# Passing weight strips through the ring of gathered rows, and keeping output and selection strips

## The chip, the cores and the metric

One NeuronCore of one Trainium2 chip runs the whole program. The metric is the time of one execution on the device in microseconds (us), here the median of the runs. TensorE is called PE, VectorE DVE, ScalarE ACT, GpSimd POOL and SyncE SP, as in the profile.

## The reference

Two layers work on 512 tokens of 1024 numbers (float32). Each layer adds a token mixer and then a channel mixer to the residual stream:

```
h = h + mixer(rms_norm(h))          # layer 0: gated linear attention, layer 1: sliding-window attention
h = h + peer_ffn(rms_norm(h))
```

A mixer is a set of projections with fixed weights around attention. The channel mixer picks, for every token and each of 8 heads, 16 of 16384 experts by a product-key search and computes, over its 128 picks e with gate g,

```
out[t] = sum_e  gelu(u[e] . x[t]) * g[t,e] * v[e]
```

Nearly all bytes come from this: each of 512 tokens reads 128 pairs (u, v) of 8 KB in each layer.

## The kernel before

The 512 tokens are four blocks of 128, so there are eight stages: four blocks in layer 0, four in layer 1. A stage serves the picks of one block while the other engines prepare the next block (its mixer, projections and expert search). That preparation is called a *prep*; it is of kind "gla" in layer 0 and "swa" in layer 1.

**Rows.** One pick of all 128 tokens is a *row*: a gather of 128 x 8 KB = 1.049 MB from the table into one slot of `ring`, which has nine slots (SLOTS). POOL issues the gathers (L666). DVE takes the dot product with h (L1094), ACT computes gelu and the coefficient (L1357, L1360) and, for most rows, a diagonal matrix (L1368), with which PE adds the v half to `acc` (L1723); for the rest of the rows DVE adds it to `side` (L1085). Whoever adds it raises the semaphore `used` of the slot, and POOL may gather the row that comes nine later. A stage has 128 rows, called row 0 to 127 below.

**Beats.** Every engine's program is one stream in which the pieces of the prep stand between rows. The table AT (not changed) says for each piece before which row, called its beat, an engine does it: for a gla prep PE does q0 at 12, q1 24, k0 29, k1 38, v0 to v3 at 43 to 52, r0 to r3 at 56 to 62, out0 to out3 at 71 to 79, pq0 to pq3 at 84 to 105; for a swa prep q0 to q3 at 13 to 22, kv 25, out0 to out3 at 75 to 87, pq0 to pq3 at 93 to 112. The prep that runs in stage 0 has later beats of its own. `beside` and `serve` weave the two. A piece whose input is late holds the rows behind it on that engine.

**Strips.** The weights of the projections are cut into strips of 256 columns, 1.049 MB each like a row: in layer 0 twenty (q0, q1, k0, k1, v0 to v3, r0 to r3, out0 to out3, pq0 to pq3, numbered 0 to 19), in layer 1 thirteen (q0 to q3, kv, out0 to out3, pq0 to pq3). "out" strips are the mixer's output projection, "pq" strips the queries of the expert search. Each is needed once in every block. Strips 0 to 8 of a layer stay in `resident` (nine places, RESIDENT). The others, 9 to 19 in layer 0 and 9 to 12 in layer 1, are fetched again for each block into a buffer of their own, `stream`, which holds one strip, in two halves (CUTS): SP issues a half (L559) as soon as PE has used the same half of the strip before. At the start of the program the ring is still empty, and strips 9 to 17 of the first block lie in it.

**SP's order.** SP issues in one order, with its waits between: streamed strips with the bias, the norm gain (after "oT") and the keys (after "y") among them (`load_streamed`, L536 on), the next block's x (`load_block`), the result of the stage before (`close`). Layer 1's resident strips come in two parts: five during stage 2 after the prep's last streamed strip (`load_kept_ahead`), four in stage 3 (`load_kept_rest`).

PE's use of a strip is in `left`, `right` and `query` (L1460, L1514, L1481); `strip`, `cut_loaded` and `cut_done` hold its waits and signals.

## Time and profile before

| | |
|---|---|
| median of 3 runs | 2897.97 us (2896.73 to 2898.08) |
| the profiled execution | 2902.58 us, its span 2900.4 us |
| PE matmul busy | 2284.9 us, 79% of the span |
| DVE busy | 2184.6 us, 75% |
| POOL busy | 1244.1 us, 43% |
| ACT busy | 1183.7 us, 41% |
| bytes by DMA | 1170.27 MB, mean 403 GB/s |
| gathered rows | 1024, 1073.81 MB, 89.7% of the DMA engines' time |
| DMAs issued by SP | 94.74 MB, 8.3% |

The span runs from the first to the last instruction of the program. A busy share is an average over the span and says nothing of when. "DMA share" is the mean busy share of the 16 DMA engines; GB/s is what they moved in a stretch. Times in the views count from the start of the span.

### The profile page before, as it was taken

How to read it: one execution, taken by the hardware profiler on the slowest of the kernel's cores; microseconds unless marked ns; L12 is line 12 of the kernel's file. 1: busy time of each engine (PE TensorE's matmuls, PEld its weight loads, DVE VectorE, ACT ScalarE, POOL GpSimd, SP SyncE). 2: the span in 40 equal slices, each digit the busy share in tenths (PEclk: the TensorE clock that was granted, in tenths of full speed). 3: DMA queues.
4: the chain of work that ended last, by engine and by line, in shares of the span. 5: the costliest groups of instructions: out<-in, count | busy, mean ns of one | idle time of the engine just before them, and what ended most of it. 6: DMA issues, size and time to landing. Idle time of an engine off the chain costs nothing.

```text
span 2900.4 us, 27200 instructions
## 1 busy us (share of the span) xinstructions
PE 2284.9 (79%) x7394; PEld 1213.3 (42%) x7394; DVE 2184.6 (75%) x5166; ACT 1183.7 (41%) x3457; POOL 1244.1 (43%) x1049
## 2 busy tenths in 40 slices
PE   9779787788877887786887878877788878886567
PEld 8536442454424554243443434443354434432122
DVE  2688678876878757796688876988679876887664
ACT  3154334344343443445344453435534453433333
POOL 0254335443444333444434543354434444345655
PEclk9899999899999898998899988989889998988989
DMA  6599999999999999999999999999999999999998
GB/s 271 209 418 421 398 398 416 421 421 403 415 420 421 420 375 420 420 418 421 421 393 406 422 421 420 389 416 421 421 402 406 421 421 421 399 421 421 422 422 350
DMA packets 170817, 1170.27 MB, mean 403 GB/s; under 512 B 19668, under 2 KB 19928, under 8 KB 36136
## 3 DMA queue, kind: packets, MB, share of 16 engines
q0 software_dynamic: 147456, 1073.81, 89.7%
q1 hardware_dynamic: 23208, 94.74, 8.3%
q8 instruction: 58, 0.95, 0.1%
q14 instruction: 95, 0.78, 0.1%
HBM read 1164.28 MB, written 4.19 MB: 403 GB/s over the span
## 4 chain that ended last, share of the span: by engine, by line
DMA 28%; DVE 14%; PE 11%; issue 6%; POOL 3%; ACT 3%; POOLq 0%; DVEq 0%; ACTq 0%
DMA ring<-in_uv,pick 26%; PE acc L1723 6%; DVE ring L1094 4%; POOL ring L666 3%; PE ps L1514 3%; DVE side L1085 1%; DMA xc<-h 1%; DMA stream<-in_strips 1%; ACT diag L1368 1%; DVE arena L969 1%; DVE arena L950 1%; DVE arena L1040 1%; DVE arena L1044 1%; DVE arena L951 1%; DVE arena L1031 1%
## 5 line engine op out<-in xcount | busy, mean ns | idle before, releaser
L666 POOL DMA_INDIRECT ring<-in_uv,pick x1024 | 1239.7, 1211 | 1630.5 <-PE acc L1723 1092.9
L1723 PE MATMUL acc<-ring,diag 128*128 128x512 f32 x2988 | 1542.5, 659 | 465.3 <-ACT diag L1368 462.3
L1094 DVE CUSTOM_DVE_ANT_0 ring<-ring,h_now 128x1024 f32<-128x1024 f32 x1024 | 1235.4, 1222 | 490.2 <-DMA ring<-in_uv,pick 474.0
L1723 PEld LDWEIGHTS acc<-ring,diag 128*128 128x128 f32 x2988 | 582.6, 207 | 1287.7 <-ACT diag L1368 702.8
L1357 ACT ACTIVATE gelu<-dots 128x1 f32<-128x1 f32 x1024 | 206.1, 201 | 1264.6 <-DVE dots L1094 1258.0
L1085 DVE SCALAR_TENSOR_TENSOR side<-ring,coef,side 128x1024 f32<-128x1024 f32 x270 | 346.0, 1281 | 23.1 <-ACT coef L1360 23.0
L1360 ACT ACTIVATE coef<-gate,gelu 128x1 f32<-128x1 f32 x1024 | 302.0, 295 | 33.2
L1368 ACT ACTIVATE diag<-ident,coef 128x128 f32<-128x128 f32 x747 | 300.1, 402 | 29.8 <-PE acc L1723 5.5
L1514 PE MATMUL ps<-resident,actT 128*128 128x256 f32 x896 | 220.3, 403 | 14.5 <-ACT actT L1169 14.5
L1514 PEld LDWEIGHTS ps<-resident,actT 128*128 128x128 f32 x896 | 178.1, 202 | 58.9 <-issue 18.2
L1481 PE MATMUL ps<-actT,stream 128*128 128x128 f32 x960 | 124.9, 291 | 23.6 <-DMA stream<-in_strips 22.7
L1481 PEld LDWEIGHTS ps<-actT,stream 128*128 128x128 f32 x960 | 121.2, 205 | 43.9 <-DMA stream<-in_strips 31.5
L1514 PE MATMUL ps<-stream,actT 128*128 128x256 f32 x336 | 96.7, 446 | 50.0 <-DMA stream<-in_strips 47.2
L1514 PEld LDWEIGHTS ps<-stream,actT 128*128 128x128 f32 x336 | 73.2, 224 | 79.4 <-DMA stream<-in_strips 62.5
L1357 ACT ACT_TABLE_LOAD x77 | 98.8, 1283 | 1.4
L1094 DVE DVE_READ_ACCUMULATOR2_ANT dots<- 128x1 f32 x1024 | 83.8, 82 | 0.0
L1305 ACT ACTIVATE arena<-ps 128x256 f32<-128x256 f32 x31 | 11.8, 381 | 126.6 <-PE ps L1481 126.6
L1460 PEld LDWEIGHTS ps<-actT,resident 128*128 128x128 f32 x512 | 59.1, 193 | 5.0 <-issue 4.5
L1460 PE MATMUL ps<-actT,resident 128*128 128x128 f32 x512 | 60.6, 277 | 0.0
L1425 PE MATMUL ps<-ident,arena 128*128 128x128 f32 x224 | 38.2, 318 | 27.6 <-DVE arena L711 15.2
L1425 PEld LDWEIGHTS ps<-ident,arena 128*128 128x128 f32 x224 | 29.9, 163 | 50.4 <-issue 26.6
L687 DVE TENSOR_SCALAR stat<-stat 128x1 f32<-128x1 f32 (+2 forms) x24 | 3.8, 160 | 61.3 <-ACT actT L1186 28.0
(198 smaller groups left out, 1454.6 us busy)
## 6 DMA issues: line engine op xcount, KB each, us to landing
stream<-in_strips SPq DMA_DIRECT2D x102, 512.0 KB
resident<-in_strips SPq DMA_DIRECT2D x18, 1024.0 KB, 12.9
ring<-in_uv,pick POOLq DMA_INDIRECT x1024
ring<-in_strips SPq DMA_DIRECT2D x9, 1024.0 KB, 19.6
arena<-in_keys SPq DMA_DIRECT2D x8, 512.0 KB
xc<-in_x SPq DMA_DIRECT2D x4, 512.0 KB
h<-arena SPq DMA_DIRECT2D x4, 512.0 KB, 11.4
xc<-h SPq DMA_DIRECT2D x4, 512.0 KB
```

The source lines that it names most:

```text
L666: pool.indirect_dma_start(ring[:, n % SLOTS, :], None, tables[layer], bass.IndirectOffsetOnAxis(ap=pick[:, col:col + 1], axis=0),).then_in ...
L950: step.mark(dve.max_index(topi[:, v, 0:8], top[:, v, 0:8], score(i)))
L1085: dve.scalar_tensor_tensor(side[:], ring[:, slot, D:2 * D], coef[:, slot:slot + 1], (side if began else xc)[:], ALU.mult, ALU.add).then_in ...
L1094: dve.tensor_tensor_reduce(ring[:, slot, 0:D], ring[:, slot, 0:D], h_now[:], 1.0, 0.0, ALU.mult, ALU.add, dots[:, slot:slot + 1]).then_inc ...
L1357: act.activation(gelu[:, slot:slot + 1], dots[:, slot:slot + 1], ACT.Gelu).then_inc(gelued, 1)
L1360: act.activation(coef[:, slot:slot + 1], gate[:, col:col + 1], ACT.Copy, scale=gelu[:, slot:slot + 1]).then_inc(weighed, 1)
L1368: act.activation(diag[:, turn % 4, :], ident[:], ACT.Copy, scale=coef[:, slot:slot + 1]).then_inc(diag_ready, 1)
L1425: i = pe.transpose(ps[:, bank + k // 4, (k % 4) * P:(k % 4 + 1) * P], src[:, k, :], ident[:])
L1460: i = pe.matmul(ps[:, bank, (2 * side + c) * P:(2 * side + c + 1) * P], w[:, k, c * P:(c + 1) * P], actT[:, k, :], start=(k == 0), stop=(k ...
L1481: i = pe.matmul(ps[:, 2 + c, (j % 2) * P:(j % 2 + 1) * P], w[:, k, c * P:(c + 1) * P], actT[:, k, :], start=(k == 0), stop=(k == KT - 1))
L1514: i = pe.matmul(dst, actT[:, k, :], w[:, k, :], start=(k == 0 and bias is None), stop=(k == KT - 1))
L1723: m = pe.matmul(acc[:, b * 512:(b + 1) * 512], diag[:, turn % 4, :], ring[:, slot, D + b * 512:D + (b + 1) * 512], start=(r == 0 and i == ...
```

## The change

`stream` and its semaphores go. The place that it had becomes a tenth place of `resident`. KEPT says which strips stay: in layer 0 v3 (7), r3 (11), out0 to out3 and pq0 to pq3; in layer 1 all but q0 to q2. The strips that don't stay (PASSING) are given places among the rows in one order over the whole program (`ring_order`): each stands one row ahead of its beat. A place's slot is its number modulo nine. SP issues a passing strip when the item nine places earlier has been used (`emptied`), PE waits for its landing and raises `used` at its last matmul, and POOL waits likewise whether the item before was a row or a strip. Strips come whole, not in halves. The signals "q" and "k" of PE in layer 0 go. SP's order becomes: for layer 0 all passing strips of the prep, then gain and keys; for layer 1 the passing strips, in its first prep then the kept strips 2 to 9 of ten (each after a row of stage 3: 24, 30, and so on to 66), then bias, gain and keys. During stage 2 two kept strips are loaded ahead instead of five. At the start of the program strips are loaded in the order of their use, strip 10 after strip 0 has been used.

```diff
-RESIDENT = 9
+KEPT = ((7, 11, 12, 13, 14, 15, 16, 17, 18, 19), (3, 4, 5, 6, 7, 8, 9, 10, 11, 12))
+RESIDENT = len(KEPT[0])
 CUTS = 2
 CUT = 8 // CUTS
-STREAMED = tuple(s - RESIDENT for s in STRIPS)
+PASSING = tuple(tuple(n for n in range(STRIPS[layer]) if n not in KEPT[layer]) for layer in range(2))
 
 PARTS = 4
 PART = HEADS_P // PARTS
-SAYS = ({11: "r", 15: "y", 16: "pq0", 17: "pq1", 18: "pq2", 19: "pq3"},
-        {8: "y", 9: "pq0", 10: "pq1", 11: "pq2", 12: "pq3"})
-DONE = [[SAYS[layer].get(n) for n in range(RESIDENT, STRIPS[layer])] for layer in range(2)]
-FREED = [[e for event in events for e in [None] * (CUTS - 1) + [event]] for events in DONE]
-GAIN_AT = (13 - RESIDENT, 10 - RESIDENT)
-AHEAD, AHEAD_AT, REST_AT = 5, 10, 5
-KEYS_AT = (16 - RESIDENT, 10 - RESIDENT)
+AHEAD, AHEAD_AT = 2, 10
+REST_AT, REST_EACH = 24, 6
...
+PIECES = (("q0", "q1", "k0", "k1", "v0", "v1", "v2", "v3", "r0", "r1", "r2", "r3", "out0", "out1", "out2", "out3",
+           "pq0", "pq1", "pq2", "pq3"),
+          ("q0", "q1", "q2", "q3", "kv", "out0", "out1", "out2", "out3", "pq0", "pq1", "pq2", "pq3"))
+def ring_order():
+    order = [(0, 0, n) for n in PASSING[0]]
+    for s in range(STAGES):
+        layer, p = divmod(s + 1, BLOCKS)
+        at = AT["first" if s == 0 else "gla" if layer == 0 else "swa"]["pe"]
+        for i in range(PICKS):
+            if s + 1 < STAGES:
+                order += [(layer, p, n) for n in PASSING[layer] if at[PIECES[layer][n]] - 1 == i]
+            order.append(s * PICKS + i)
+    return {item: place for place, item in enumerate(order)}
+PLACE = ring_order()
+def slot_of(item):
+    return PLACE[item] % SLOTS
+def turn_of(item):
+    return PLACE[item] // SLOTS
+def landings():
+    seen = {(kind, slot): 0 for kind in ("strip", "pick") for slot in range(SLOTS)}
+    count = {}
+    for item in sorted(PLACE, key=PLACE.get):
+        key = ("strip" if isinstance(item, tuple) else "pick", slot_of(item))
+        seen[key] += 1
+        count[item] = seen[key]
+    return count
+LANDED = landings()
...
-        stream = sb("stream", [P, KT, STRIP])
...
-            if n < RESIDENT:
-                return resident[:, n]
-            if in_ring(prep, n):
-                return ring[:, n - RESIDENT, :].rearrange("p (k c) -> p k c", k=KT)
-            return stream
+            if not passing(prep, n):
+                return resident[:, KEPT[prep.layer].index(n)]
+            return ring[:, slot_of((prep.layer, prep.p, n)), :].rearrange("p (k c) -> p k c", k=KT)
...
-            eng.wait_ge(used[n % SLOTS], n // SLOTS + 1)
+            eng.wait_ge(used[slot_of(n)], turn_of(n) + 1)
+        def emptied(eng, item):
+            if turn_of(item):
+                eng.wait_ge(used[slot_of(item)], turn_of(item))
...
-                said_by(sp, "pe", before(prep), "v")
+                said_by(sp, "pe", before(prep), "r")
                 for n in range(AHEAD):
                     released(sp, pick_number(BLOCKS - 2, AHEAD_AT + n - 1, 0))
@@ -524,45 +549,44 @@
                 said_by(sp, "pe", prep, "q")
                 for n in range(AHEAD, RESIDENT):
-                    released(sp, pick_number(BLOCKS - 1, REST_AT + n - AHEAD - 1, 0))
+                    released(sp, pick_number(BLOCKS - 1, 0, REST_AT + (n - AHEAD) * REST_EACH))
                     load_kept(prep, n)
+            def load_passing(prep, n):
+                item = (prep.layer, prep.p, n)
+                emptied(sp, item)
+                sp.dma_start(ring[:, slot_of(item), :], strips[prep.layer][n])\
+                  .then_inc(strip_got[slot_of(item)], 16)
             def load_streamed(prep):
                 if prep.layer == 1:
+                    for n in PASSING[1]:
+                        if n < out0(prep):
+                            load_passing(prep, n)
+                    if prep.first:
+                        load_kept_rest(prep)
                     said_by(sp, "pe", prep, "o3")
                     sp.dma_start(bias_out, b_out).then_inc(bias_loaded, 16)
-                opening = prep.first and prep.layer == 0
-                if opening:
-                    for n in range(SLOTS):
-                        sp.dma_start(ring[:, n, :], strips[0][RESIDENT + n]).then_inc(ring_loaded[n], 16)
-                for n in range(STREAMED[prep.layer]):
-                    if n == GAIN_AT[prep.layer]:
-                        said_by(sp, "pe", prep, "oT")
-                        if prep.layer == 0:
-                            said_by(sp, "dve", prep, "state1")
-                        sp.dma_start(ffn_gain, gain_ffn[prep.layer:prep.layer + 1, :]).then_inc(gain_loaded, 16)
-                    if n == KEYS_AT[prep.layer]:
-                        said_by(sp, "pe", prep, "y")
-                        sp.dma_start(keysT, (keys0, keys1)[prep.layer]).then_inc(keys_loaded, 16)
-                    for c in range(CUTS):
-                        if opening and n < SLOTS:
-                            break
-                        if n > (SLOTS if opening else 0):
-                            freed(prep, (n - 1) * CUTS + c)
-                        elif not opening:
-                            freed(before(prep), (STREAMED[before(prep).layer] - 1) * CUTS + c)
-                        sp.dma_start(stream[:, c * CUT:(c + 1) * CUT, :].rearrange("p k c -> p (k c)"),
-                                     strips[prep.layer][RESIDENT + n, :, c * CUT * STRIP:(c + 1) * CUT * STRIP])\
-                          .then_inc(slot_loaded[c], 16)
+                elif not prep.first:
+                    for n in PASSING[0]:
+                        load_passing(prep, n)
+                said_by(sp, "pe", prep, "oT")
+                if prep.layer == 0:
+                    said_by(sp, "dve", prep, "state1")
+                sp.dma_start(ffn_gain, gain_ffn[prep.layer:prep.layer + 1, :]).then_inc(gain_loaded, 16)
+                if prep.layer == 1:
+                    for n in PASSING[1]:
+                        if n >= out0(prep):
+                            load_passing(prep, n)
+                said_by(sp, "pe", prep, "y")
+                sp.dma_start(keysT, (keys0, keys1)[prep.layer]).then_inc(keys_loaded, 16)
...
-            for n in range(RESIDENT):
-                load_kept(Prep("gla", 0), n)
+            def load_opening(begin, end):
+                for n in range(begin, end):
+                    if n in KEPT[0]:
+                        load_kept(Prep("gla", 0), KEPT[0].index(n))
+                    else:
+                        load_passing(Prep("gla", 0), n)
+            load_opening(0, 9)
             for dst, src in ((ggla[:], gla_gain),
                              (gqk[:].rearrange("p a d -> p (a d)"), qk_gain.to_broadcast([P, 2 * HD])),
                              (sink[:], sinks.to_broadcast([P, HEADS_Q])), (posi, positions)):
                 sp.dma_start(dst, src).then_inc(consts_late, 16)
+            load_opening(9, STRIPS[0])
...
-                    if n >= SLOTS:
-                        released(pool, n - SLOTS)
-                        alone(pool, passed["pool"])
-                    elif SAYS[0].get(RESIDENT + n, "r") not in ("r", "y", "pq0"):
-                        said_by(pool, "pe", Prep("gla", 0), SAYS[0][RESIDENT + n])
-                        alone(pool, passed["pool"])
+                    emptied(pool, n)
+                    alone(pool, passed["pool"])
                     col = n - layer * BLOCKS * PICKS
                     pool.indirect_dma_start(
-                        ring[:, n % SLOTS, :], None, tables[layer],
+                        ring[:, slot_of(n), :], None, tables[layer],
                         bass.IndirectOffsetOnAxis(ap=pick[:, col:col + 1], axis=0),
-                    ).then_inc(got[n % SLOTS], 16)
+                    ).then_inc(got[slot_of(n)], 16)
...
-                said_by(dve, "pe", prep, "k")
+                released(dve, (0, prep.p, 3))
...
-                if n < RESIDENT and prep.first:
-                    pe.wait_ge(res_loaded[n], 16 * (prep.layer + 1))
+                if passing(prep, n):
+                    item = (prep.layer, prep.p, n)
+                    pe.wait_ge(strip_got[slot_of(item)], LANDED[item] * 16)
+                elif prep.first:
+                    pe.wait_ge(res_loaded[KEPT[prep.layer].index(n)], 16 * (prep.layer + 1))
                 return weight(prep, n)
-            def cut_loaded(prep, n, c):
-                if in_ring(prep, n):
-                    pe.wait_ge(ring_loaded[n - RESIDENT], 16)
-                elif n >= RESIDENT:
-                    pe.wait_ge(slot_loaded[c], prep.slot_uses(n - RESIDENT) * 16)
-            def cut_done(n, c, ins):
-                if n >= RESIDENT and c < CUTS - 1:
-                    used_up(ins)
+            def strip_done(prep, n, ins):
+                if passing(prep, n):
+                    ins.then_inc(used[slot_of((prep.layer, prep.p, n))], 1)
```

## Rows read from the trace of the kernel before

**Rows 1.** The page: busy, GB/s of 40 equal slices, bytes.
```profile
PE 2284.9 (79%) x7394; PEld 1213.3 (42%) x7394; DVE 2184.6 (75%) x5166; ACT 1183.7 (41%) x3457; POOL 1244.1 (43%) x1049
...
GB/s 271 209 418 421 398 398 416 421 421 403 415 420 421 420 375 420 420 418 421 421 393 406 422 421 420 389 416 421 421 402 406 421 421 421 399 421 421 422 422 350
```

**Rows 2.** Stretches: us, busy of PE, PEld, DVE, ACT, POOL, PEclk, DMA share, GB/s.
```profile
50.00:108.20 58.20, 53.82 (x312) 43.10 (x311) 19.36 (x75) 12.28 (x32) 0.00 (x0) 1.00 0.14 47
...
345.00:450.00 105.00, 84.74 (x318) 50.11 (x319) 79.19 (x238) 36.55 (x102) 38.80 (x34) 0.93 0.98 388
450.00:650.00 200.00, 158.48 (x495) 84.06 (x495) 159.52 (x326) 82.28 (x241) 87.73 (x75) 0.89 1.01 420
650.00:745.00 95.00, 76.99 (x302) 45.00 (x301) 59.78 (x133) 37.15 (x108) 36.20 (x31) 1.00 1.00 403
745.00:990.00 245.00, 190.30 (x619) 99.42 (x618) 203.62 (x479) 102.74 (x299) 111.41 (x94) 0.92 1.01 421
990.00:1090.00 100.00, 82.93 (x283) 49.64 (x282) 57.77 (x98) 38.57 (x113) 35.00 (x30) 0.91 0.98 387
...
1460.00:1600.00 140.00, 111.30 (x372) 58.15 (x373) 120.60 (x376) 61.32 (x179) 55.99 (x51) 0.93 1.00 399
...
1790.00:1860.00 70.00, 58.27 (x231) 32.32 (x231) 59.42 (x192) 29.85 (x80) 23.37 (x22) 0.98 0.97 392
...
2140.00:2190.00 50.00, 41.85 (x174) 25.87 (x173) 41.34 (x156) 19.45 (x54) 14.81 (x15) 0.90 0.96 375
...
2480.00:2540.00 60.00, 53.08 (x217) 30.82 (x216) 53.64 (x197) 25.49 (x71) 21.75 (x20) 0.93 0.99 394
```

**Rows 3.** Waits of PE: total us, times, longest; last row 1460 to 2540 us alone.
```profile
PE ps L1514 <- DMA stream<-in_strips: 47.2, 22, 5.5
...
PE ps L1481 <- DMA stream<-in_strips: 22.7, 15, 3.2
...
PE ps L1481 <- DMA stream<-in_strips: 12.9, 7, 3.2
```

**Rows 4.** Order of time from 345 us, idle before in brackets; then one stretch.
```profile
349.67 6.25 PE L1514 MATMUL ps<-stream,actT 128*128 128x256 f32 x16 [5.48 <-DMA stream<-in_strips]
...
358.45 0.94 POOL L666 DMA_INDIRECT ring<-in_uv,pick  x1 [10.36 <-PE acc L1723]
...
352.50:362.50 10.00, 9.25 (x33) 6.71 (x32) 4.57 (x7) 1.80 (x6) 1.88 (x2) 0.88 0.73 263
```

**Rows 5.** The page: DMA issues, count, KB each, us to landing.
```profile
stream<-in_strips SPq DMA_DIRECT2D x102, 512.0 KB
resident<-in_strips SPq DMA_DIRECT2D x18, 1024.0 KB, 12.9
...
ring<-in_strips SPq DMA_DIRECT2D x9, 1024.0 KB, 19.6
```

**Rows 6.** SP's issues from 1730 to 1850 us: start, us.
```profile
1734.48 0.83 SPq L559 DMA_DIRECT2D stream<-in_strips  x2
...
1805.48 31.50 SPq L559 DMA_DIRECT2D stream<-in_strips  x6
```

**Rows 7.** One stretch: all engines; then only DVE's dot products (L1094).
```profile
1785.00:1840.00 55.00, 46.03 (x202) 29.04 (x201) 43.61 (x137) 21.24 (x58) 15.59 (x14) 0.94 0.96 386
...
1785.00:1840.00 55.00, 19.28 (x32) 0.94 0.96 386
```

**Rows 8.** The chain of waits in stage 7: start, us, what.
```profile
2717.25 17.26 DMA ring<-in_uv,pick
...
2736.82 3.31 PE acc L1723 x4
```

**Rows 9.** Order of time: PE's matmuls of one strip; one gather by POOL.
```profile
601.77 3.62 PE L1514 MATMUL ps<-resident,actT 128*128 128x256 f32 x16
...
1581.15 1.12 POOL L666 DMA_INDIRECT ring<-in_uv,pick  x1 [10.59 <-PE acc L1723]
```

More of the change, by code:

```diff
@@ L206, in value @@
         return self.p * len(names) + (base + names.index(event) + 1)
-    def strips_used(self, n):
-        per = [f.count(None) for f in FREED]
-        before = 0 if self.layer == 0 else BLOCKS * per[0]
-        return self.p * per[self.layer] + (before + FREED[self.layer][:n + 1].count(None))
-    def slot_uses(self, n):
-        return self.p * STREAMED[self.layer] + (n + 1 + (0 if self.layer == 0 else BLOCKS * STREAMED[0])) - SLOTS
 def alone(eng, passed):
@@ L319, in build @@
         res_loaded = [sem(f"res_loaded{i}") for i in range(RESIDENT)]
-        slot_loaded = [sem(f"slot_loaded{c}") for c in range(CUTS)]
-        ring_loaded = [sem(f"ring_loaded{i}") for i in range(SLOTS)]
-        strip_used = sem("strip_used")
+        strip_got = [sem(f"strip_got{s}") for s in range(SLOTS)]
         consts_loaded = sem("consts_loaded")
@@ L414, in before, with passing @@
             return Prep(prep.kind, prep.p - 1)
-        def in_ring(prep, n):
-            return prep.first and prep.layer == 0 and RESIDENT <= n < RESIDENT + SLOTS
+        def passing(prep, n):
+            return n in PASSING[prep.layer]
         def weight(prep, n):
-            if n < RESIDENT:
-                return resident[:, n]
-            if in_ring(prep, n):
-                return ring[:, n - RESIDENT, :].rearrange("p (k c) -> p k c", k=KT)
-            return stream
+            if not passing(prep, n):
+                return resident[:, KEPT[prep.layer].index(n)]
+            return ring[:, slot_of((prep.layer, prep.p, n)), :].rearrange("p (k c) -> p k c", k=KT)
         def out0(prep):
@@ L479, in _ @@
         def _(sp):
-            def freed(prep, n):
-                event = FREED[prep.layer][n]
-                if event is None:
-                    sp.wait_ge(strip_used, prep.strips_used(n))
-                else:
-                    said_by(sp, "pe", prep, event)
             def load_block(prep):
@@ L1469, in query @@
                 for cut in range(CUTS):
-                    cut_loaded(prep, n, cut)
                     if j == 0:
@@ L1474, in query @@
                         i = query_part(w, j, c, cut)
-                    cut_done(n, cut, i)
                 return i
@@ L1488, in first_head @@
                 for cut in range(CUTS):
-                    cut_loaded(prep, pq0(prep), cut)
                     said_by(pe, "act", prep, ("h2T_a", "h2T")[cut])
@@ L1500, in first_head @@
                     i = query_part(w, 0, 1, cut)
-                    cut_done(pq0(prep), cut, i)
                 return i
@@ L1536, in gla @@
                 yield at["q1"]
-                say(left(prep, 1, 2, 1))
+                left(prep, 1, 2, 1)
                 yield at["k0"]
@@ L1546, in gla @@
                 yield at["k1"]
-                say(left(prep, 3, 3, 1))
+                left(prep, 3, 3, 1)
                 for n in range(4):
@@ L1719, in part @@
                         n = pick_number(s, r, i)
-                        slot, turn = n % SLOTS, TURN_OF[n]
+                        slot, turn = slot_of(n), TURN_OF[n]
                         pe.wait_ge(diag_ready, turn + 1)
```

31 lines of the change are left out of this document (11 added, 20 removed).

## The prediction

> **What bounds the kernel now.** I read the slices of the page first, since they say whether any resource is full. In [rows 1] the line of GB/s stands at 420 to 422 in most slices and sinks to between 375 and 406 once a stage, for one to three slices, and it is low (271, 209) in the first two. PE is busy 79% and DVE 75% of the span, so none of the engines is full for long, and the DMA is. The second view is the table of stretches [rows 2], cut at the edges of those dips. Outside a dip the DMA moves 421 GB/s (745 to 990 us), so one row or one strip of 1.049 MB costs 1.049/421 = 2.49 us of the DMA. In a dip the rate is 375 to 403. What a dip leaves unused is its length times (1 - rate/421): 8.2, 4.1 and 8.1 us in the three of layer 0, together 20.4 us; 7.3, 4.8, 5.5 and 3.8 us in the four of layer 1, together 21.4 us. From 50 to 108 us the DMA is nearly empty (share 0.14), PE alone is at work.
>
> So the time is a sum: bytes at 421 GB/s, plus what is left unused. A change of the bytes counts in full only where the DMA is full. The third view is who waits [rows 3]: PE sat idle 47.2 + 22.7 = 69.9 us for a streamed strip, of which 12.9 us lie in layer 1 (1460 to 2540 us), so 57.0 us in the three dips of layer 0. The fourth view shows how that reaches the DMA [rows 4]: PE waits 5.48 us for a strip, the rows behind it aren't added, POOL waits 10.36 us for a free slot of the ring, and the DMA runs at 263 GB/s for 10 us.
>
> **The change, term by term.** All prices are from the profiled execution, which took 2902.6 us for a span of 2900.4; the median of the runs is 2898.0, 4.6 us less, and the sum is taken off that.
>
> *Fewer strips.* Before, 51 strips were streamed in halves, 18 loaded to stay and 9 put in the ring at the start [rows 5]: 78. Afterwards, layer 0 passes 10 strips four times and keeps 10, layer 1 passes 3 four times and keeps 10: 72. Six strips at 2.49 us are -14.9 us. All six fall after 145 us, where the DMA is mostly full.
>
> *The opening.* Twenty strips are loaded before and after. Strips 18 and 19 came late through the single buffer, beside an almost empty DMA, and now come at the start. Strip 10 must wait until strip 0 has been used, long before it is needed. PE covers both: 0 us, at most 2 us either way.
>
> *Layer 0: output and selection strips stay.* In its three dips PE had to be fed r3, out0 to out3 and pq0 to pq3 through a buffer that holds one strip. Now they lie in SBUF. This does two things. PE loses 57.0 us of waiting. But the DMA also loses the transfers that it had in the dips: eight strips in each of three, 24 x 2.49 = 59.8 us, and the strips that replace them (q, k, v, r) pass in the stretches before, where the DMA is full. If the waiting of PE is all that goes, the unused time grows by 59.8 - 57.0 = 2.8 us. If the rows, no longer sharing the DMA, also come in time for everything else, all 20.4 us go. I take the middle, -10 us. Beyond half I don't dare: in the dips PE is busy over 80% of the time (82.9 of the 100 us from 990 on, [rows 2]), so PE is itself near its limit.
>
> *Layer 1: selection strips stay.* Of the four streamed strips one is fetched early, at 1734 us, in a full stretch, and three (six halves) are fetched from 1805 us on, in the dip [rows 6]. Four stages lose three such transfers each from the dip: 12 x 2.49 = 29.9 us. PE gains 12.9 us there. The rest is PE's and DVE's own work: from 1785 to 1840 us DVE served 16 rows (32 instructions, two per row), which are 39.8 us of the DMA, while PE was busy 46.0 us [rows 7]. So PE can't follow the rows at 2.49 us each, and the strips that were fetched meanwhile were free. Taking them out of the dip leaves up to 29.9 - 12.9 = 17.0 us more unused; at least 0, if PE catches up. I take +13, since 46.0 is over 39.8 and the ring of nine can hide only part of it.
>
> *Strips in the ring.* Nine slots now carry, after the opening, rows and 42 passing strips (three times ten in layer 0, four times three in layer 1). The trace of before has no strip between rows, so I bound the price. A slot comes round every 9 x 2.49 = 22.4 us. A row of the quiet last stage spent 17.26 us from issue to landing, most of it queued behind other rows, and PE was through with the next one 3.31 us after its start [rows 8]. A strip holds its slot for 3.62 us of PE more [rows 9], and this fits into the queueing time: lower bound 0. Upper bound: each strip delays the issue behind it by its 3.62 us and the DMA loses what it lost in [rows 4], 1 - 263/421 = 0.38 of it, 42 x 3.62 x 0.38 = 58 us. I take +3 us, near the quiet row, because in the stretches where the strips pass POOL has several rows queued; only r0 to r2 (beside the attention steps) and q0 to q2 of layer 1 (POOL already waits 10.59 us at 1581 us, [rows 9]) are tight.
>
> *Loads that stay, and SP's queue.* Layer 1's ten kept strips are fetched two in stage 2 and eight in stage 3 instead of five and four, no more in all than the bytes above count. Before, q to kv came in a burst; now each waits for a row of stage 3 (24, 30, ... 66), and out0, the first needed, waits for row 24 and is used at beat 75: 0 us. Behind the waiting strip on SP stand the bias, gain and key loads and the next block's x; the last passing strip of layer 0 (r2) is issued when about row 52 is through, the gain waits for oT at beat 69 anyway: 0 us. Events "q" and "k" that go, and the wait that moves to the strip's own slot, end at the same matmul: 0 us.
>
> *Whole strips for halves.* With half strips in the mix the DMA moves 420 GB/s (450 to 650 us), without them 421 [rows 2]: 51 strips x 2.49 us x 1/421 is 0.3 us, counted as nothing. The Trainium skill (SBUF — State Buffer, The DMA setup-cost knee) gives every DMA a fixed cost of about 2 us; taken one after another, an estimate from it would be a gain of 2 us for every strip that is no longer cut, some 90 us. This trace doesn't agree, since 420 against 421 shows that with other transfers queued the fixed part is hidden.
>
> Sum: -14.9 + 0 - 10 + 13 + 3 = -8.9 us, 2898.0 - 8.9 = 2889 us.
>
> **Rivals.**
> *The waits were the cause of the dips (A).* Then layer 0 returns its 20.4 us, and layer 1's PE catches up (0 instead of +13). For it: the chain of [rows 4] is plain to see. Against: PE at 83% in the dips of layer 0 and 84% (46.0 of 55) in layer 1's. Time: 2898.0 - 14.9 - 20.4 + 3 = 2866 us. The Trainium skill's rule to issue a DMA early and wait for it late (DMA: Bandwidth & Descriptors, Rules for kernel authors) points to this case.
> *The saving is taken back by free transfers made dear (B).* Layer 0 gives only 2 us, layer 1 costs 12, and the 3 us of the ring stand: 2898.0 - 14.9 - 2 + 12 + 3 = 2896 us, no change that can be told.
> *The ring is too short (C), slower.* The place is the ring during v0 to r2 of layer 0 and q0 to q2 of layer 1: two or three of nine slots hold strips that wait for PE, POOL waits, the DMA runs dry. Price: half of the upper bound, 29 us instead of 3, with everything else as forecast: 2889 + 26 = 2915 us. It decides from 3 + 8.9 = 12 us in all on, 0.28 us per passing strip. For it: a strip is given a slot nine places ahead though it is needed only at its turn. The Trainium skill (DMA: Bandwidth & Descriptors, Queues, rings and completion order) says that an engine of the DMA goes round between its queues; by that a strip issued on SP's queue overtakes the rows queued by POOL and lies in its slot early, idle. No run here shows it yet. Against: the 17.26 us of queueing, which is the reserve.
>
> **How the numbers follow.** A measurement here can tell 0.2%, 5.8 us, from no change, so faster means under 2892.2 and slower over 2903.8. The forecast (2880 to 2896) has 0.38, A 0.20, B 0.22, C 0.20. The faster share is A and most of the forecast, 0.20 + 0.31 = 0.51. Same is the rest of the forecast and most of B, 0.25. Slower is C and a little of B, 0.24. The range goes from 2870, nearly A, to 2909, short of C.
>
> **What would show it.** After 145 us the dips of layer 0 should leave about 10 us unused instead of 20, with no wait of PE for a strip over 1 us. The dips of layer 1 should be deeper: under 380 GB/s instead of 375 to 399, with POOL waiting for PE. Between the dips, where the strips now pass, 419 GB/s or more; if it is below 415 there, the ring is too short and C holds. A strip count other than 72 in the list of issues, or a wait of POOL for a strip's matmul over 5 us outside the dips, would prove the sum wrong at once.

## The result and the profile after

The changed kernel takes 2913.63 us (median of five runs, 2910.98 to 2919.22) against 2897.97 us (five runs, 2895.62 to 2902.91): 1.0055 times the time before, 95% interval 1.0041 to 1.007. It is slower by about 16 us, where 9 us less were forecast. The profiled execution after took 2910.98 us with a span of 2908.9 us, so the two profiles differ by 8.5 us and not by 16. The one before lies 4.6 us above its median, the one after 2.6 us below. What follows explains the 8.5 us; the rest can't be read from these two traces.

The page of the kernel after, as [rows 1] and [rows 5] show it of before: busy time, GB/s of 40 slices, all bytes, and the DMA issues (count, KB each, us from issue to landing).

```profile
PE 2282.7 (78%) x7394; PEld 1212.1 (42%) x7394; DVE 2184.7 (75%) x5166; ACT 1183.3 (41%) x3457; POOL 1253.4 (43%) x1049
...
GB/s 299 185 421 410 414 369 408 421 414 409 397 421 421 411 421 397 422 421 421 421 358 422 417 421 418 363 422 418 421 383 400 403 421 421 373 421 421 422 421 356
...
DMA packets 162610, 1163.99 MB, mean 400 GB/s; under 512 B 18756, under 2 KB 19016, under 8 KB 22168
...
ring<-in_strips SPq DMA_DIRECT2D x52, 1024.0 KB, 9.4
resident<-in_strips SPq DMA_DIRECT2D x20, 1024.0 KB, 15.5
...
ring<-in_uv,pick POOLq DMA_INDIRECT x1024, 14.0
```

The engines do the same work in nearly the same time. The strips are 52 + 20 = 72, six fewer. But four of the sunken slices are deeper: 369, 358, 363 and 373 where before had 398, 393, 389 and 399. (The fifteenth, 375 before, is full now, and the one behind it has sunk from 420 to 397.) The next fence cuts the stretches out, as [rows 2] does (us; busy of PE, PEld, DVE, ACT, POOL; granted clock of PE; DMA share; GB/s).

```profile
345.00:450.00 105.00, 91.73 (x363) 54.31 (x364) 91.70 (x253) 47.68 (x139) 42.47 (x37) 0.97 0.95 372
450.00:650.00 200.00, 143.92 (x430) 72.09 (x429) 147.16 (x320) 76.50 (x221) 82.51 (x68) 0.86 1.01 418
650.00:745.00 95.00, 90.26 (x359) 57.42 (x358) 70.29 (x129) 42.91 (x128) 44.69 (x36) 0.98 1.00 412
745.00:990.00 245.00, 185.92 (x572) 93.29 (x571) 192.17 (x479) 96.31 (x278) 103.06 (x89) 0.89 1.00 414
990.00:1090.00 100.00, 89.48 (x337) 56.06 (x335) 71.12 (x118) 43.27 (x127) 42.80 (x36) 0.97 1.00 413
1470.00:1520.00 50.00, 45.03 (x181) 25.46 (x179) 46.83 (x171) 21.14 (x60) 20.26 (x18) 0.93 0.86 330
1790.00:1860.00 70.00, 58.49 (x220) 33.53 (x219) 60.38 (x194) 30.21 (x82) 23.76 (x21) 0.90 0.91 357
2150.00:2200.00 50.00, 43.28 (x176) 24.85 (x175) 44.17 (x165) 20.90 (x61) 17.52 (x16) 0.91 0.87 336
2500.00:2540.00 40.00, 33.61 (x126) 18.65 (x126) 37.36 (x154) 16.37 (x44) 16.37 (x15) 0.91 0.85 334
1600.00:1730.00 130.00, 99.25 (x306) 50.20 (x304) 103.78 (x207) 65.37 (x188) 63.63 (x53) 0.93 1.01 419
```

Three of these stretches are cut closer than those of [rows 2]; in the kernel before the same ones are:

```profile
1470.00:1520.00 50.00, 40.60 (x155) 22.01 (x153) 44.67 (x166) 20.19 (x57) 18.41 (x17) 0.97 0.98 383
...
2150.00:2200.00 50.00, 40.50 (x142) 22.74 (x142) 43.70 (x164) 19.96 (x56) 17.42 (x16) 0.90 0.96 378
2500.00:2540.00 40.00, 36.31 (x138) 19.07 (x137) 38.63 (x144) 19.97 (x56) 17.41 (x16) 1.00 0.98 390
```

In layer 1 every dip falls: 383 to 330, 392 to 357, 378 to 336, 390 to 334. In layer 0 the first dip sinks (388 to 372), and inside the windows of [rows 2] the two later ones rise (403 to 412, 387 to 413). But they haven't filled. They have moved behind the edge of the window, as two stretches show, first of before, then of after:

```profile
745.00:820.00 75.00, 62.10 (x191) 29.83 (x190) 69.18 (x225) 33.69 (x96) 33.95 (x29) 0.93 1.01 420
1090.00:1180.00 90.00, 67.60 (x217) 34.22 (x216) 72.51 (x256) 28.62 (x85) 30.23 (x29) 0.89 1.01 420
```
```profile
745.00:820.00 75.00, 61.31 (x193) 29.79 (x192) 72.51 (x246) 32.66 (x93) 32.74 (x29) 0.93 0.98 398
1090.00:1180.00 90.00, 71.59 (x243) 36.22 (x242) 82.24 (x274) 37.65 (x111) 37.27 (x33) 0.92 0.99 402
```

What POOL waits for is next (us in total, times, longest).

```profile
POOL ring L692 <- PE acc L1732: 957.7, 413, 15.0
...
POOL ring L692 <- DVE side L1111: 219.1, 111, 8.3
POOL ring L692 <- PE ps L1528: 113.6, 26, 11.1
...
POOL ring L692 <- PE ps L1479: 33.3, 8, 6.1
```

PE no longer waits for any strip; the 69.9 us of [rows 3] are gone. POOL now waits 146.9 us in 34 places for a strip's matmuls (L1528, L1479), for example this gather in a full stretch:

```profile
613.61 1.89 POOL L692 DMA_INDIRECT ring<-in_uv,pick  x1 [11.11 <-PE ps L1528]
```

I add the time up by bytes, since edges of fixed windows fall differently in the two kernels. Four lines of the view of the DMA follow: layer 0 of before, from row 16 of stage 0 to row 16 of stage 3 (159.6 to 1246.2 us by their landings), layer 1 of before up to row 0 of stage 7 (to 2569.7 us), then the same two of after (158.7 to 1243.2, and to 2579.1 us).

```profile
DMA packets 66981, 448.04 MB, mean 412 GB/s; under 512 B 7477, under 2 KB 7478, under 8 KB 17130
DMA packets 78156, 547.23 MB, mean 413 GB/s; under 512 B 8690, under 2 KB 8693, under 8 KB 14080
```
```profile
DMA packets 61798, 444.93 MB, mean 410 GB/s; under 512 B 6897, under 2 KB 6898, under 8 KB 8102
DMA packets 75406, 543.99 MB, mean 407 GB/s; under 512 B 8384, under 2 KB 8387, under 8 KB 9678
```

Length less MB/421 GB/s is the time left unused. Layer 0: 1086.6 - 1064.2 = 22.4 us before, 1084.5 - 1056.8 = 27.7 after. Layer 1: 1323.5 - 1299.8 = 23.7 before, 1335.9 - 1292.1 = 43.8 after. So the opening gives -1, the bytes give 6.35 MB/421 = -15.1, layer 0 costs 5.3 and layer 1 costs 20.1: together +9.3 us, which is what row 0 of stage 7 is later (2579.1 against 2569.7), and nearly what the span grew (8.5).

### The profile page after: what moved, and what is told of

Its sections match the earlier page's. It is cut to its first block, busy times and chain, and to the rows that moved or that the text cites. A ratio compares the mean times of both kernels' runs of the same rounds, so it can differ in the third digit from the quotient of the medians.

```text
span 2908.9 us, 27136 instructions
## 1 busy us (share of the span) xinstructions
PE 2282.7 (78%) x7394; PEld 1212.1 (42%) x7394; DVE 2184.7 (75%) x5166; ACT 1183.3 (41%) x3457; POOL 1253.4 (43%) x1049
## 4 chain that ended last, share of the span: by engine, by line
DMA 27%; DVE 16%; PE 10%; issue 6%; ACT 3%; POOL 3%; POOLq 0%; DVEq 0%; ACTq 0%
DMA ring<-in_uv,pick 26%; PE acc L1732 6%; DVE ring L1120 5%; POOL ring L692 3%; PE ps L1528 2%; DVE side L1111 1%; DMA xc<-h 1%; DVE arena L995 1%; DVE arena L976 1%; ACT diag L1394 1%; DVE arena L1066 1%; DVE arena L1070 1%; DVE arena L977 1%; DVE arena L1057 1%; ACT coef L1386 1%
## 5 line engine op out<-in xcount | busy, mean ns | idle before, releaser
L1732 PE MATMUL acc<-ring,diag 128*128 128x512 f32 x2988 | 1568.8, 669 | 519.7 <-ACT diag L1394 518.9
L692 POOL DMA_INDIRECT ring<-in_uv,pick x1024 | 1249.0, 1220 | 1629.6 <-PE acc L1732 957.7
L1528 PE MATMUL ps<-resident,actT 128*128 128x256 f32 x768 | 178.1, 386 | 11.1 <-ACT actT L1195 7.3
L1528 PEld LDWEIGHTS ps<-resident,actT 128*128 128x128 f32 x768 | 145.2, 192 | 47.2 <-issue 18.8
L1528 PE MATMUL ps<-ring,actT 128*128 128x256 f32 x576 | 135.6, 392 | 0.0
L1499 PEld LDWEIGHTS ps<-actT,resident 128*128 128x128 f32 x1024 | 125.4, 200 | 21.4 <-issue 17.2
L1499 PE MATMUL ps<-actT,resident 128*128 128x128 f32 x1024 | 125.6, 283 | 3.3 <-ACT actT L1195 3.2
L1528 PEld LDWEIGHTS ps<-ring,actT 128*128 128x128 f32 x576 | 112.5, 198 | 27.4 <-issue 12.5
L1479 PEld LDWEIGHTS ps<-actT,ring 128*128 128x128 f32 x512 | 59.4, 193 | 5.3 <-issue 4.8
L1479 PE MATMUL ps<-actT,ring 128*128 128x128 f32 x512 | 60.6, 277 | 0.0
```

What stands on the lines that cost most here:

```text
L692: pool.indirect_dma_start(ring[:, slot_of(n), :], None, tables[layer], bass.IndirectOffsetOnAxis(ap=pick[:, col:col + 1], axis=0),).then_i ...
L1479: i = pe.matmul(ps[:, bank, (2 * side + c) * P:(2 * side + c + 1) * P], w[:, k, c * P:(c + 1) * P], actT[:, k, :], start=(k == 0), stop=(k ...
L1499: i = pe.matmul(ps[:, 2 + c, (j % 2) * P:(j % 2 + 1) * P], w[:, k, c * P:(c + 1) * P], actT[:, k, :], start=(k == 0), stop=(k == KT - 1))
L1528: i = pe.matmul(dst, actT[:, k, :], w[:, k, :], start=(k == 0 and bias is None), stop=(k == KT - 1))
L1732: m = pe.matmul(acc[:, b * 512:(b + 1) * 512], diag[:, turn % 4, :], ring[:, slot, D + b * 512:D + (b + 1) * 512], start=(r == 0 and i == ...
```

## The experiments

Two theories stood against each other. *Displacement* (rival B, stronger): the buffer that went had been fed in the dips, where the rows can't use the DMA, so its strips were nearly free, and now all strips pass where the DMA is full. *Short ring* (rival C): strips hold slots and the rows come late. Each time below is a median; the kernel before, run beside, had 2899.4 to 2901.6 us, where it had 2898.0 beside after. So a difference between one of these kernels and after is good to about 4 us only; the ratios in brackets are against the kernel before, run beside.

**none.** No strip passes after the opening; a kept one is read in its place.
```
-                order += [(layer, p, n) for n in PASSING[layer] if at[PIECES[layer][n]] - 1 == i]
+                order += []
...
-                return resident[:, KEPT[prep.layer].index(n)]
+                return resident[:, KEPT[prep.layer].index(n) if n in KEPT[prep.layer] else 0]
```


> The changed kernel in which no strip passes after the opening: the 42 fetches of passing strips are left out (PE reads a kept strip in their place, so the output is not the reference's), and the ring carries rows alone. Two theories. Displacement: the strips now pass where the DMA is full, each costs its 2.49 us there and nothing more, and the dips are short of transfers because PE and DVE set the pace in them. Then 42 x 2.49 = 105 us go: 2913.6 - 105 = 2809 us, and the dips of layer 1 stay as deep as in the changed kernel. Short ring: a passing strip costs more than its transfer because it holds a slot; at 0.3 to 0.6 us each more, the time is 2784 to 2796 us. Against the kernel before, the same run prices its 49 streamed strips after the opening (122 us of transfers): displacement says they cost clearly less than that, about 2898 - 2809 = 89 us.

Measured 2805.09 us (0.968, 0.9664 to 0.9695). The 42 passing strips cost 2913.6 - 2805.1 = 108.5 us, 2.58 each, where the DMA needs 2.49 for one: hardly more than the bytes. The kernel before moves 48 strips more than this one (1170.27 - 1119.94 = 50.3 MB) and pays 2899.4 - 2805.1 = 94.3 us, 1.96 us each. That is the heart of the case: the old path had a discount of 0.5 us per strip, 25 us in all (48 x 2.49 = 119.5, less 94.3). In layer 1 (1161.3 to 2473.5 us) the dips are there without any passing strip:

```profile
DMA packets 74122, 534.65 MB, mean 407 GB/s; under 512 B 8240, under 2 KB 8243, under 8 KB 9534
```

1312.2 - 1270.0 = 42.2 us unused, against 43.8 in after; in layer 0, worked out alike (410.27 MB from 158.3 to 1161.3 us), 28.5 against 27.7. So the ring's strips did not make the holes in after. This is how deep they are when nothing but rows is there to fill them.

**hybrid.** Layer 1 goes back to streaming its last four strips in halves, through one place of the resident buffer, so outside the ring; layer 0 stays as in after. This kernel fetches 75 strips, three more than after.
```
-KEPT = (..., (3, 4, 5, 6, 7, 8, 9, 10, 11, 12))
+KEPT = (..., (0, 1, 2, 3, 4, 5, 6, 7, 8))
-PASSING = tuple(tuple(n for n in range(STRIPS[layer]) if n not in KEPT[layer]) for layer in range(2))
+PASSING = (tuple(n for n in range(STRIPS[0]) if n not in KEPT[0]), ())
+            def load_stream(prep, j):
...
```


> Layer 0 as in the changed kernel (ten kept strips, ten passing through the ring), layer 1 as in the kernel before: nine kept, and the selection strips streamed in halves into the tenth place of resident, a buffer outside the ring. 75 strips. Displacement (the dips are set by PE and DVE, and only transfers outside the ring can use them): layer 1 comes back to the unused time of before (24 us instead of 44 from stage 3 on), layer 0 stays 5 us worse and three strips (7.5 us) cheaper than before: 2898 - 7.5 + 5.4 = 2896 us, under the changed kernel by 18. If the ring's passing strips were what slows the changed kernel, layer 0 with its 30 passes would keep most of the loss: 2908 us or more.

Measured 2897.02 us (11 runs; 0.9987, 0.9978 to 0.9996). Layer 1's part alone is worth 16.6 us against after, though it moves three strips more. Two of its dips, and its bytes over layer 1 (1244.3 to 2565.2 us):

```profile
1790.00:1860.00 70.00, 57.17 (x232) 32.00 (x231) 61.36 (x210) 29.23 (x78) 25.31 (x22) 0.95 1.00 403
2140.00:2190.00 50.00, 40.02 (x170) 22.89 (x169) 42.66 (x161) 19.24 (x55) 17.71 (x16) 0.97 0.94 375
```
```profile
DMA packets 78147, 547.19 MB, mean 414 GB/s; under 512 B 8686, under 2 KB 8689, under 8 KB 14076
```

403 GB/s from 1790 us on instead of 357, 375 at 2140 as in [rows 2], and 1320.9 - 1299.7 = 21.2 us unused. DVE is busy no less in the stretch (61.36 us against 60.38), so nothing shows that the strips slow the rows down there.

**before_thin and after_thin.** The price of a transfer by its place. In before, the second to fourth streamed strip of each stage of layer 1 fetch 64 columns a half; in after, the passing strips of layer 1 fetch 128 of 2048 columns. Each takes away nearly all bytes of 12 strips (11.8 MB, 28 us of the DMA); all waits and signals stay, and the output isn't the reference's.
```
+                        if prep.layer == 1 and n:    # before_thin
+                            sp.dma_start(stream[:, c * CUT, 0:64],
+                                         strips[1][RESIDENT + n, :, c * CUT * STRIP:c * CUT * STRIP + 64])\
...
+                if prep.layer == 1:                  # after_thin
+                    sp.dma_start(ring[:, slot_of(item), 0:128], strips[1][n, :, 0:128])
```


> The kernel before, in which the streamed strips pq1, pq2 and pq3 of layer 1 (three in each of four preps, 12 in all) are fetched only in a sliver (64 of 1024 columns' worth of each half), so the output is not the reference's; all waits and signals stay. It takes 12 x 2.49 = 30 us of transfers, less a sixteenth, out of the dips of layer 1. Displacement: PE and DVE set the pace there, the unused time of layer 1 rises from 24 us towards the 44 us of the changed kernel, and only about 10 us go: 2889 us. If the DMA or the waiting for strips sets the pace in the dips, 28 us or more go: 2871 us or less.

> The changed kernel, in which the passing strips q0, q1 and q2 of layer 1 (three in each of four preps, also 12) are fetched only in a sliver, the waits, slots and signals kept (the output is not the reference's). Displacement: they pass where the DMA is full, so all their transfer time goes, 28 to 30 us: 2884 us, about three times what the same number of strips gives in the kernel before. If passing strips are as cheap as the streamed ones were, 10 us: 2904 us.

Measured 2891.55 us (0.9968, 0.9958 to 0.9979) and 2892.84 us (0.9972, 0.9961 to 0.9984). The same 28 us are worth 8.4 us in the dips of before and 20.8 us in the full stretches of after (9 and 24 by the ratios). Two lines show where the rest went: layer 1 of before_thin (1247.4 to 2559.5 us) and of after_thin (1236.7 to 2557.4 us).

```profile
DMA packets 78149, 535.41 MB, mean 408 GB/s; under 512 B 11759, under 2 KB 11762, under 8 KB 14077
```
```profile
DMA packets 75417, 535.23 MB, mean 405 GB/s; under 512 B 8384, under 2 KB 9539, under 8 KB 10830
```

Before_thin leaves 1312.1 - 1271.8 = 40.3 us unused, 16.6 more than before: emptied, its dips are nearly those of after. After_thin leaves 1320.7 - 1271.3 = 49.4, 5.6 more than after (three of its twelve transfers fall ahead of this window), so even in the full stretches a strip doesn't return all of its 2.49 us.

A third theory is that TensorE's granted clock made the dips: from 1790 to 1860 us it is 0.98 in before and 0.90 in after. Before_thin speaks against it. Here are its last dip and that of before; the clock is 1.00 and 0.97, and it is the emptied dip that sinks:

```profile
2490.00:2550.00 60.00, 51.65 (x185) 26.17 (x183) 58.20 (x212) 28.39 (x79) 25.68 (x23) 1.00 0.94 369
```
```profile
2490.00:2550.00 60.00, 53.08 (x208) 29.49 (x205) 56.04 (x219) 24.52 (x72) 23.16 (x22) 0.97 0.99 396
```

**late.** A passing strip gets its place three rows later, so it holds its slot for a shorter time.
```
-  ... if at[PIECES[layer][n]] - 1 == i]
+  ... if at[PIECES[layer][n]] + 2 == i]
```


> The changed kernel with every passing strip placed three rows later in the ring's order (two rows behind its beat's row instead of one ahead), so that it holds its slot about 3 x 2.49 = 7.5 us less. Bytes and everything else are the same. Displacement: the holding costs almost nothing in the changed kernel (42 x 2.58 us measured for 42 x 2.49 of bytes), so 2911 to 2914 us, no change. Short ring: 10 us less, 2904 us.

Measured 2912.49 us (1.0045, 1.0031 to 1.0059), 1.1 us below after (3 by the ratios): a shorter hold gives nothing that can be told. POOL now waits for no strip at all, and that much longer for rows:

```profile
POOL ring L692 <- PE acc L1732: 1040.2, 443, 15.0
...
POOL ring L692 <- DVE side L1111: 285.9, 131, 7.6
```

That is 1326.1 us of waiting, against 957.7 + 219.1 + 146.9 = 1323.7 in after. The strip was only the last name on a wait that was there anyway. With none, this rules out the short ring as the main cause here; at most the 4 us of 42 x (2.58 - 2.49) are left for it.

**swap1, swap0, swap01, late01, before8.** The other way round: the ring carries the strips of the dips, and the early strips stay. swap1 keeps strips 0 to 9 of layer 1 and passes the last three selection strips (pq1 to pq3), swap0 keeps 0 to 7, 11 and 15 of layer 0 and passes r0 to r2, out0 to out2 and the four selection strips, swap01 does both, late01 is swap01 with the edit of late; the loads of SP are moved to fit, and one small matmul more follows each passing selection strip to carry its event. before8 is the kernel before with a ring of eight.
```
-KEPT = ((7, 11, 12, 13, 14, 15, 16, 17, 18, 19), (3, 4, 5, 6, 7, 8, 9, 10, 11, 12))
+KEPT = (..., (0, 1, 2, 3, 4, 5, 6, 7, 8, 9))    # swap1
+KEPT = ((0, 1, 2, 3, 4, 5, 6, 7, 11, 15), ...)  # swap0
-SLOTS = 9
+SLOTS = 8                                       # before8
```


> The changed kernel, but in layer 1 strips pq1, pq2, pq3 pass through the ring and q0, q1, q2 are kept (five strips loaded ahead in stage 2, five in stage 3). The bytes are the same, layer 0 is the same. Displacement: three transfers a stage go back from a full stretch into the dip of layer 1, whose unused time should fall from about 10 to about 5 us a stage: 2913.6 - 4 x 4.5 = 2896 us. Short ring: in the dip the rows wait longest for PE, so a slot held by a strip there costs most: 2914 us or more.

> The changed kernel, but in layer 0 the strips r0 to r2, out0 to out2 and pq0 to pq3 pass through the ring and q, k, v, r3 and out3 are kept. The bytes are the same, layer 1 is the same. Displacement: seven transfers a block move into the dips of layer 0; the unused time of layer 0 (28 us from row 16 of stage 0 to row 16 of stage 3) should fall by 10 us or more: 2904 us or less. Short ring: two or three slots are held while PE is at its busiest, the dips get deeper: 2918 us or more.

> Both moves of passing strips at once, in layer 0 and layer 1, at the same bytes as the changed kernel. Displacement: the sum of the two gains, 2913.6 - 18 - 10 = 2886 us, under both kernels. Short ring: the sum of the two losses, 2918 us or more.

> The kernel in which the passing strips are those of the dips in both layers (swap01, 2943 us), with the strips placed three rows later. In the dips PE is behind and slots are scarce. If the loss of swap01 against the changed kernel (30 us) is the holding of slots in the dips, a shorter holding gives back a third to a half: 2928 to 2933 us. If the loss is the PE work or the order of loads that the move added, it stays 2940 or more.

> The kernel before with eight slots in the ring instead of nine, all else the same: the price of one slot. In the dips PE holds rows for 20 to 28 us after they land, against 22.4 us for a turn of nine slots, so one slot less, 2.49 us, should deepen each of seven dips by about 2.5 us: 2899 + 17 = 2916 us. If the dips are not limited by slots, 2899 us. In the full stretches a row is used about 9 us after landing, no loss is expected there.

Measured: swap1 2923.13 us (1.0081, 1.0066 to 1.0096), swap0 2932.38 (1.0115, 1.0098 to 1.0133), swap01 2943.31 (1.0147, 1.0128 to 1.0165), late01 2921.39 (1.0077, 1.0061 to 1.0092), before8 2926.02 (1.009, 1.0073 to 1.0107). I had expected from displacement that strips put back into the dips would be cheap. They are not, when they go through the ring: against after the three swaps lose 9.5, 18.8 and 29.7 us. What POOL waits for in swap0, then in swap1, points at the reason (for strips in all 174.6 and 190.2 us, where after has 146.9):

```profile
POOL ring L699 <- PE ps L1542: 94.9, 26, 17.4
POOL ring L699 <- PE ps L1513: 79.7, 10, 14.9
```
```profile
POOL ring L691 <- PE ps L1505: 97.9, 12, 17.6
```

In a dip PE is behind, so a strip lies in its slot until PE comes to it, and POOL waits for the slot 15 to 18 us in the worst places, where the worst of after is 11.1. before8 shows what a slot is worth: one of nine less costs 26 us. Late01, which has swap01's extra matmuls and order of loads too, gets 21.9 of its 29.7 us back by three rows' delay, so the loss was mostly the holding of slots. So a short ring is a real danger of this design, but after, whose strips pass between the dips, doesn't meet it. What the old path had, and hybrid has again in layer 1, was both at once: DMA time in the dip and a place that was none of the nine.

**after_light, after_dve, after_both.** What keeps the rows from filling the dips of layer 1? after_light halves the selection strips' matmuls of layer 1, after_dve lets the dot products of rows 88 to 127 of stages 3 to 6 read a quarter of their columns, after_both does both.
```
+                        if cut == 0 or prep.layer == 0:
+                            i = query_part(w, j, c, cut, KT if prep.layer == 0 else CUT)
...
+                        wide = D // 4 if BLOCKS - 1 <= s < STAGES - 1 and 8 * r + i >= 88 else D
```


> The changed kernel, in which PE does only the first half of the sums of the four selection strips of layer 1 (64 of 128 matmuls a prep left out, 16 for each strip, about 1.9 us each strip, 7.6 us a prep; the output is not the reference's). Bytes, rows and ring are the same. If PE sets the pace in the dips of layer 1, the unused time of each shrinks by up to 7.6 us: 2913.6 - 4 x 5 = 2894 us or less. If DVE's selection work behind it sets the pace, or the DMA does, little changes: 2908 to 2914 us.

> The changed kernel, in which DVE takes the dot product of rows 88 to 127 of stages 3 to 6 over 256 of 1024 columns (so the output is not the reference's): about 0.9 us less DVE work for each of 160 rows, 36 us a stage, just in and behind the dips of layer 1. Bytes, gathers and PE's work are the same. If DVE (its selection work between the rows) sets the pace in the dips, their unused time, 10.6 us each, falls by more than half: 2913.6 - 4 x 6 = 2890 us or less. If the chain through PE, ACT and DVE in turn sets it, with no one engine short, 2900 to 2908 us. If DVE has nothing to do with it, 2914 us.

> Both relieved, PE's half sums of the selection strips of layer 1 (as in after_light) and DVE's narrow dot products (as in after_dve). If the two engines together set the pace, the four dips of layer 1 go nearly altogether, 42 us: 2875 us. If only DVE does, no better than after_dve by itself.

Measured 2908.89 us (1.0028, 1.0018 to 1.0038), 2908.64 (1.0022, 1.0013 to 1.0031) and 2897.72 (0.9989, 0.998 to 0.9998). Against after that is -4.7, -5.0 and -15.9 us by the medians, -8, -10 and -19 by the ratios. The dip from 1790 us in the three, in this order:

```profile
1790.00:1860.00 70.00, 55.47 (x184) 30.56 (x182) 60.35 (x192) 29.12 (x79) 23.17 (x22) 0.88 0.91 366
```
```profile
1790.00:1860.00 70.00, 63.02 (x246) 37.05 (x245) 45.76 (x205) 31.20 (x86) 21.80 (x23) 0.94 0.90 367
```
```profile
1790.00:1860.00 70.00, 59.44 (x210) 33.10 (x209) 46.21 (x209) 31.21 (x86) 22.80 (x24) 0.91 0.93 376
```

357 becomes 366, 367 and 376 GB/s. Neither engine alone sets the pace; both together gain at least the sum of the two, 16 to 19 us, where after leaves 44 unused in layer 1. For the two engines as the whole limit I had expected 2875 us. So more than half of the holes isn't explained by these edits, and what keeps it open was not found.

**best.** hybrid's layer 1 with swap0's layer 0 and late's order.
```
+KEPT = ((0, 1, 2, 3, 4, 5, 6, 7, 11, 15), (0, 1, 2, 3, 4, 5, 6, 7, 8))
+  ... if at[PIECES[layer][n]] + 2 == i]
```


> A version made of what the runs showed: layer 1 streams its selection strips into the tenth place as in hybrid; layer 0 passes r0 to r2, out0 to out2 and pq0 to pq3 through the ring and keeps the rest, each placed three rows later. In late01 this layer 0 stood 5 us under the kernel before at row 16 of stage 3, and hybrid's layer 1 gains 3 us more from there: 2899.5 - 8 = 2891 us. If late placing in the dips helps only by chance of that one profile, it is no better than hybrid, 2897 us.

Measured 2898.7 us (11 runs; 0.9993, 0.9984 to 1.0001), where 2891 were hoped for: no better than hybrid, which is the fastest complete kernel of the study, by 0.13% under the one before.

## Why the prediction was wrong

- *Fewer strips* (-14.9): right, -15.1 by the bytes.
- *The opening* (0, at most 2): right, -1 us (row 16 lands at 158.7 against 159.6 us).
- *Layer 0: output and selection strips stay* (-10): **this step failed.** Measured +5.3 us. I had let the rows fill half of what the dips left unused once PE's waiting was gone, and they filled nothing. Around the first dip (345 to 450 us) 12.2 us are unused instead of 8.3. From 650 to 820 us, the second dip with what lies behind it, it is 6.2 instead of 4.1, and from 990 to 1180 us 5.9 instead of 8.2; the larger part of both holes (4.1 and 4.0 us) now lies about 100 us later, where before moved 420 GB/s. The last 2.6 us are unused ahead of 345 and between 450 and 650 us. None says the same: with rows alone layer 0 leaves 28.5 us. The waits of [rows 3] are all gone, so the chain of [rows 4] was real, but without it the rows ran into another limit. I took the middle of two bounds although PE was at 81 and 83% in the two later dips; in the same windows it is at 95 and 89% now. In the holes themselves it is DVE that is nearly full (third busy time):

```profile
760.00:800.00 40.00, 34.94 (x119) 18.15 (x118) 38.99 (x127) 18.41 (x53) 17.26 (x15) 0.91 0.96 378
1120.00:1160.00 40.00, 34.98 (x114) 17.66 (x113) 39.02 (x129) 18.41 (x53) 18.33 (x16) 0.91 0.97 378
```

  That DVE makes these holes isn't shown: before has it at 38.69 us from 760 to 800 and still moves 420 GB/s. No run of layer 0 settles it. The bound of +2.8 was misread besides. It put all 57.0 us of waiting into the three dips. Cut by the windows of [rows 2] (345, 650, 990 us, in this order) they hold 14.2 + 15.8 + 14.9 = 44.9 us:

```profile
PE ps L1514 <- DMA stream<-in_strips: 10.0, 3, 5.5
...
PE ps L1481 <- DMA stream<-in_strips: 4.2, 4, 1.5
```
```profile
PE ps L1514 <- DMA stream<-in_strips: 13.6, 8, 2.6
...
PE ps L1481 <- DMA stream<-in_strips: 2.2, 2, 1.7
```
```profile
PE ps L1514 <- DMA stream<-in_strips: 14.9, 6, 3.9
```

  The other 12 us fell outside them, where the DMA was nearly full. With 44.9 the step's own reckoning reads 59.8 - 44.9 = +14.9 instead of +2.8, and the measured +5.3 lies well inside it. The Trainium skill has the rule to issue a DMA early and wait for it late (DMA: Bandwidth & Descriptors, Rules for kernel authors). In this case's trace no wait of PE for a strip is left, and the kernel is no faster for it.
- *Layer 1: selection strips stay* (+13): the direction was right, the size too small. Measured +20.1. Of these 3.4 fell from 2271 to 2316 us (17.52 MB), outside a dip; the rest is about the bound of the step, 17.0. before_thin gives the same by another way, 16.6 us of 28 not returned. The reduction from 17 to 13, for what nine slots could hide, had no measurement behind it.
- *Strips in the ring* (+3): about right. none leaves as much unused as after, and late gains 1.1 us. Yet two of the signs that I had set for a short ring came out. One was a wait of POOL over 5 us for a strip's matmul outside a dip (11.11 us at 613.61), and it would have misled: the DMA still moved 418 GB/s from 450 to 650 us. The other was under 415 GB/s between the dips (414 from 745 to 990 us), and it misleads too: the loss there lies between 745 and 820 us, and SP issues no strip from 641.3 to 846.8 us. The bound of 58 us is what the swaps went towards.
- *Loads that stay* (0): nothing in the traces speaks against it. *Whole strips for halves* (0): the size stands, the argument doesn't. The two stretches compared, 450 to 650 and 745 to 990 us, hold six and five half strips, so 420 against 421 GB/s tells nothing. What speaks against a gain of 90 us is that before leaves only 22.4 + 23.7 = 46.1 us unused over both layers.

The sum with measured terms is -15.1 - 1 + 5.3 + 20.1 = +9.3 us, against -8.9 forecast. Rival B was the right mechanism: it had 10 us for the two layers, and 25.4 were measured. Rival C gave 2915 us, which the result hit, but none and late show that its mechanism isn't what happened; the number agreed by chance. C's premise did come true: strips overtake rows. A strip that SP issued at 565.7 us took 9.1 us to land, while the gathers that POOL had issued at 563.1 and 564.3 us took 15.0 and 16.3 (medians over the kernel: 9.4 and 14.0). The Trainium skill (DMA: Bandwidth & Descriptors, Queues, rings and completion order) says that the DMA's engines go round between the queues, and this agrees.

Left open: 7 us of the 16 between the medians, which the profiled executions don't show, what holds the rows in the moved holes of layer 0, and what beside PE and DVE does in the dips of layer 1. The discount of 25 us from none and 48 strips is the better measure of the whole, since it rests on medians: -15 us for the bytes, +25 for the discount lost, +4 for the passing (42 x (2.58 - 2.49)) make +14.

## What to carry to other kernels

Price a transfer by what the DMA does at the moment when it runs, not by its bytes: in a stretch that the engines bound it may cost a third of its time (8.4 of 28 us), in a full one three quarters or more. Before a buffer is taken away, ask which idle time of the DMA it alone could fill, and what can fill it afterwards. A wait for a DMA on the busiest engine can be worth nothing: here 57 us of it went in layer 0, and the holes came back about 100 us later. Look behind the edges of the windows before calling a dip filled. And take the transfers out of the dip in a trial (before_thin) before rebuilding the kernel for it.

## What the runs showed of the hardware

- One of nine ring slots of 1 MB is worth 26 us of 2900 here (before8), while holding slots for three rows longer costs between 1 us (after against late) and 22 us (swap01 against late01), by whether the strips fall between the dips or into them.
- DMAs of two queues don't land in the order of their issue: at the same size a strip from SP's queue, issued at 565.7 us, landed at 574.8, ahead of gathers that POOL had issued at 563.1 and 564.3 us and that took 15.0 and 16.3 us.
